# First gate unit taken into the last recurrence head, and early splitting of the merged tiles

## The chip, the cores and the metric

One core of one Trainium2 chip runs the whole program. The metric is device time in microseconds (us) of one execution. The kernel drives its five engines by hand: TensorE (PE in the rows, its weight loads PEld), VectorE (DVE), ScalarE (ACT), GpSimd (POOL) and SyncE (SP, which only starts transfers). Each engine has its own instruction stream; the streams meet through semaphores. Matmul results go to PSUM, of which there are 8 banks of 512 fp32 columns on 128 partitions.

## The reference

One layer of a decoder trunk over 1088 tokens (T: a prompt of L = 1024, and 8 samples of 8) with model width 1024 (KD = 8 tiles of 128 channels). What matters here is the part between the recurrence and the output projection:

```python
# token_mixer, cut
hq, hf, hi, hg, fq, fk, fv, ff, mg = jnp.split(h @ lw['w_in'], SPLIT_IDX, axis=-1)
o_h, s_new = hgrn_chunked(...)                      # 4 heads, state 128x128
o_h = rmsnorm(o_h, lw['hg_onorm']) * jax.nn.silu(hg)
br_h = o_h.reshape(B, L, HG_WIDTH) @ lw['w_br_h']   # 512 -> 1024
...
br_f = o_f.reshape(B, L, FOX_WIDTH) @ lw['w_br_f']  # 512 -> 1024
g_h, g_f = jnp.split(jax.nn.sigmoid(mg), N_BRANCH, axis=-1)
y = (g_h * br_h + g_f * br_f) @ lw['w_out']
```

Around it, `layer` computes the modulation `mod = silu(c) @ ada_w + ada_b` for 9 conditions, two norms, and a squared-ReLU MLP. Everything is fp32.

## The kernel before, in words

Activations lie channel-major: a tile is 128 channels by 1088 tokens. An fp32 product is made from three products of split operands, high x high, low x high and high x low. ScalarE makes a high part by a copy to fp32r (`split_hi`, L255), VectorE a low part by a subtraction (`split_lo`, L261). The projection from `w_in` is cut into **units** of 128 output channels: 8 k-tiles, each of 9 matmuls (3 products in 3 column pieces), 72 matmuls at L273 in `channel_tile`. Weights of a unit are loaded by SP into `w_raw` (two slots, L449), split into `w_hi` and `w_lo` (two slots), and the result stands in one of two accumulators: `acc(0)` lies in PSUM banks 0 to 2, `acc(1)` in banks 3 to 5. Semaphores count units: `w_hi_ready`, `w_lo_ready`, `unit_done` (PE), `acc_read` (the accumulator was read).

The program has phases with a barrier between them (`phase_end`: the engine drains, raises its count, and, unless `wait=False`, waits for the other three).

**Phase 4, the recurrence**: 4 heads (`head`). In a head, PE projects units 1 to 3 of the head, transposes, runs the chunked recurrence (L1933 to L1966), then, in the heads 0 to 2, projects the first unit of the next head, while ACT sums the squares of the last token block, DVE (L1462), POOL (L730, the power -0.5) and DVE again (L1464, L1466) make the norm and raise `hn_ready`. Then PE transposes the normed tokens into bank 2 and banks 6 and 7 (L1975, L1977), and DVE multiplies them with the output gate into `mix` (L1473, 64 and 1024 columns). The last head (`last_one=True`) has no next unit and projects nothing there. POOL stores the states by DMA and waits for that before it ends its phase.

**Phase 5, the merge** (`merge_pair` on PE, ACT and DVE): 8 steps `d`, one for each channel tile, in pairs `it` with `dd` 0 and 1; three pairs in a loop (`Fori`), the last one written out. A step on PE is: gate unit 0 (for `g_h`) into `acc(0)`, branch product 0 (`br_h`, L2026) into `acc(1)`, gate unit 1 (`g_f`) into `acc(0)`, branch product 1 into `acc(1)`, and a small transpose (L2043). After each half of a gate unit comes a `mod_pair` (L2001), small matmuls for the modulation, whose weights POOL loads in 512 KB pieces into two buffers (L758); piece i is loaded when piece i-2 was used. `gate` begins with

```python
pe.wait_ge(w_lo_ready, n + 1)
pe.wait_ge(w_hi_ready, n + 1)
pe.wait_ge(acc_read, n)        # every accumulator before this one was read
```

ACT applies the sigmoid (L1034), DVE multiplies the branch product with it (L1501) and adds the two (L1503) into `merged[:, d]`. Before the first step PE waits for all engines' phase 4 and for `c_spread`, which POOL raises after it has started four branch-weight transfers (L746, L747) and spread the conditions (L753).

**End of phase 5**: after the last step ACT copies the eight merged tiles to `h_hi` (L1051), DVE subtracts for `h_lo` (L1516, `merged_split`). `h_hi` and `h_lo` hold the input of the gate units until then. PE starts phase 6 without a barrier: the output projection (L2057, `out_step`) takes k-tile by k-tile for the first four token tiles (s = 0 to 3: 6 matmuls of 512 columns each; y of tile s stands in banks 2s and 2s+1), and for each k waits for `merged_split` and the split weights. The weights of k = 0 and 1 are split ahead; those of k = 2 to 7 are split by ACT and DVE in phase 6, after the barrier, and k = 4 to 7 are loaded by SP after it, between the loads of x and of the norm rows (L507 to L513).

**Lines that the prediction's steps touch**: `merge_pair` of ACT, DVE and PE, `head` of DVE and PE, `gate`, `branch`, the loop over k of the output projection.

Of the kernel before, what the change touches and what calls it, by code (L numbers as in the profile page):

```python
# [15 lines left out]
F32 = mybir.dt.float32  # L16
# [4 lines left out]
ACT = mybir.ActivationFunctionType  # L21
# [8 lines left out]
def build_layer(nc, x_prompt, x_sample, c_prompt, c_sample, cache_k, cache_v, cache_logf, state_hgrn, page_table,  # L30
# [8 lines left out]
    KD = D // P  # L39
# [53 lines left out]
    with ExitStack() as ctx:  # L93
# [739 lines left out]
        def _(act):  # L833
# [159 lines left out]
            with act.Fori(0, HH) as h:  # L993
                hi(U_HG, 4, h, 1)
                act.wait_ge(unit_done, 4 * h + (U_HG + 1))
                a0 = acc(U_HG % 2)
                ACTIVATE(hK, a0, ACT.Sigmoid, scale=-1.0)
                ACTIVATE(hF, a0, ACT.Sigmoid)
                act.drain().then_inc(acc_read, 1)
                hi(U_HG, 4, h, 2)  # L1000
                act.wait_ge(unit_done, 4 * h + (U_HG + 2))
                ACTIVATE(hQ, acc((U_HG + 1) % 2), ACT.Copy, scale=float(DK) ** -0.5).then_inc(acc_read, 1)
                act.wait_ge(f_ready, h + 1)
                ACTIVATE(hF, hF, ACT.Ln).then_inc(g_ready, 1)
                hi(U_HG, 4, h, 3)
                act.wait_ge(unit_done, 4 * h + (U_HG + 3))
                ACTIVATE(hV, acc(U_HG % 2), ACT.Copy).then_inc(acc_read, 1)
                act.wait_ge(b_ready, h + 1)
                ACTIVATE(hE, hB, ACT.Exp)
                ACTIVATE(hN, hB, ACT.Exp, scale=-1.0)  # L1010
                act.drain().then_inc(eb_ready, 1)
                hi(U_HG, 4, h, 4)
                act.wait_ge(unit_done, 4 * h + (U_HG + 4))
                ACTIVATE(hS, acc((U_HG + 1) % 2), ACT.Silu).then_inc(acc_read, 1)
                for t in range(NT + 1):
                    r = P if t < NT else TS
                    act.wait_ge(ho_ready, (NT + 1) * h + t + 1)
                    ACTIVATE(h_otok[0:r, t, :], bank(4 + t % 2 if t < NT else 6, 0, P, rows=r), ACT.Copy).then_inc(ho_copied, 1)
                    act.drain()
                    ACTIVATE(hF[0:r, P * (t % 2):P * (t % 2) + P], h_otok[0:r, t, :],  # L1020
                             ACT.Square, accum_out=h_ms[0:r, t:t + 1])
                act.drain().then_inc(hss_ready, 1)
            phase_end(act, "act", 4)


            act.sem_inc(mod_copied, 1)

            def merge_pair(it, last=False):
                for dd in range(2):
                    for j, dst in enumerate((gate_h, gate_f)):  # L1030
                        hi(U_MG, 4, it, 2 * dd + j + 1)
                        n, slot, _ = number(U_MG, 4, it, 2 * dd + j)
                        act.wait_ge(unit_done, n + 1)
                        ACTIVATE(dst, acc(0), ACT.Sigmoid).then_inc(acc_read, 1)  # L1034
                    if last and dd:
                        hi(U_OUT, 0, 0, 1)
                        act.wait_ge(rows_tr, 1)
                        ACTIVATE(rows_T, bank(7, P, 4 * P, rows=KD * NC), ACT.Copy)
                        act.drain()
                        act.dma_start(rows_dram[:, 0:3, :], rows_T.rearrange("p (v x) -> p v x", x=P))\  # L1040
                            .then_inc(rows_stored, 16)
                    act.wait_ge(ada_used, 8 * it + (KD + 4 * dd + 4))
                    act.wait_ge(mod_tr, 2 * it + dd + 1)
                    ACTIVATE(mod_cols, bank(6, 0, P), ACT.Copy).then_inc(mod_copied, 1)
                    act.wait_ge(br_added, 2 * it + dd + 1)

            with act.Fori(0, KD // 2 - 1) as it:
                merge_pair(it)
            merge_pair(KD // 2 - 1, last=True)
            for d in range(KD):  # L1050
                ACTIVATE(h_hi[:, d, :], merged[:, d, :], ACT.Copy).then_inc(h_raw, 1)  # L1051
            phase_end(act, "act", 5)


# [96 lines left out]
        def _(dve):  # L1151
# [246 lines left out]
            def head(h, last=False):  # L1398
# [66 lines left out]
                                h_ms[:, 0:NT].unsqueeze(2).broadcast_to([P, NT, DV]), ALU.mult)  # L1465
                v.tensor_scalar(h_otok[0:TS, NT, :], h_otok[0:TS, NT, :], h_ms[0:TS, NT:NT + 1], None, ALU.mult)  # L1466
                dve.drain().then_inc(hn_ready, 1)
                if not last:
                    lo(U_HG, 4, h, 5)
                mixed_head = mix[:, bass.ds(h + G, 1), :].rearrange("p a b -> p (a b)")  # L1470
                for i, (a, b, src) in enumerate(((L, T, bank(2, 0, TS)), (0, L, psum[:, 3072:3072 + L]))):
                    dve.wait_ge(ho_tr, 2 * h + i + 1)
# [10 lines left out]
            dve.sem_inc(mod_added, 1)  # L1483
            dve.sem_inc(br_read, 1)

            def merge_pair(it, last=False):
                for dd in range(2):
                    d = 2 * it + dd
                    lo(U_MG, 4, it, 2 * dd + 1)
                    lo(U_MG, 4, it, 2 * dd + 2)  # L1490
                    dst = merged[:, bass.ds(d, 1), :].rearrange("p a b -> p (a b)")
                    if last and dd:
                        times_norm(post1, 2, V_P1, False)
                        times_norm(pre2, 4, V_N2, True)
                        dve.drain().then_inc(rows_calc, 1)
                    for j, (out, gate) in enumerate(((dst, gate_h), (gate_f, gate_f))):
                        if last and dd and j:
                            lo(U_OUT, 0, 0, 1)
                        dve.wait_ge(acc_read, 4 * it + (U_MG + 2 * dd + j + 1))
                        dve.wait_ge(br_ready, 4 * it + (2 * dd + j + 1))  # L1500
                        v.tensor_mul(out, acc(1), gate).then_inc(br_read, 1)  # L1501
# [9 lines left out]
            with dve.Fori(0, KD // 2 - 1) as it:  # L1511
                merge_pair(it)
            merge_pair(KD // 2 - 1, last=True)
            for d in range(KD):
                dve.wait_ge(h_raw, KD + d + 1)
                v.tensor_sub(h_lo[:, d, :], merged[:, d, :], h_hi[:, d, :].bitcast(F32)).then_inc(merged_split, 1)  # L1516
            phase_end(dve, "dve", 5)


# [140 lines left out]
        def _(pe):  # L1660
# [249 lines left out]


            pe.wait_ge(hg_zeroed, 1)
            def head(h, last_one=False):
                for j in range(1, 4):
                    n, slot, _ = number(U_HG, 4, h, j)
                    project(pe, n, slot)
# [49 lines left out]
                    last = mm(bank(6, 0, P, rows=TS), q_by_b[:, b, :], s_states[:, b, :], start=False,  # L1966
                              stop=(b == NB - 1))
                last.then_inc(ho_ready, 1)
                if not last_one:
                    pe.wait_ge(ho_copied, (NT + 1) * h + NT)  # L1970
                    n, slot, _ = number(U_HG, 4, h, 4)
                    project(pe, n, slot)
                pe.wait_ge(hn_ready, h + 1)
                past_waits(pe, "pe")
                tr(bank(2, 0, TS), h_otok[0:TS, NT, :], ident[0:TS, 0:TS]).then_inc(ho_tr, 1)  # L1975
# [5 lines left out]
            project(pe, U_HG, U_HG % 2)  # L1981
            with pe.Fori(0, HH - 1) as h:
                head(h)
            head(HH - 1, last_one=True)
            phase_end(pe, "pe", 4)


            pe.wait_ge(c_spread, 1)
            pe.sem_inc(mod_tr, 1)

            def merge_pair(it, last_pair=False):
                for dd in range(2):
                    d = 2 * it + dd
                    def mod_pair(i):
# [10 lines left out]
                    def gate(j):  # L2005
# [5 lines left out]
                        for k in range(KD):  # L2011
                            last = channel_tile(slot, 0, k)
                            if k == KD - 1:
                                last.then_inc(unit_done, 1)
                            if k % 4 == 3:
                                mod_pair(2 * j + k // 4)

                    def branch(j):

                        w_br = br_raw[dd].rearrange("p (k n) -> p k n", n=P)  # L2020
                        if j == 0:
                            pe.wait_ge(br_landed[dd], 32 * it + 32)
                        pe.wait_ge(br_read, 4 * it + (2 * dd + j + 1))
                        for k in range(4):
                            for a, b in PIECES:
                                last = mm(acc(1)[:, a:b], w_br[:, 4 * j + k, :], mix[:, (G, 0)[j] + k, a:b],  # L2026
                                          start=(k == 0), stop=(k == 3))
                        last.then_inc(br_ready, 1)

                    gate(0)  # L2030
                    branch(0)
                    gate(1)
                    if last_pair and dd:
                        pe.wait_ge(mod_added, d + 1)
                        pe.wait_ge(rows_calc, 1)
# [6 lines left out]
                    pe.wait_ge(mod_added, d + 1)  # L2042
                    tr(bank(7, 0, P), mod_cols, ident[:, :]).then_inc(mod_tr, 1)  # L2043

            with pe.Fori(0, KD // 2 - 1) as it:
                merge_pair(it)
            merge_pair(KD // 2 - 1, last_pair=True)
            phase_end(pe, "pe", 5, wait=False)
# [25 lines left out]
            for k in range(KD):  # L2074
                pe.wait_ge(merged_split, k + 1)
                pe.wait_ge(w_lo_ready, U_OUT + k + 1)
                pe.wait_ge(w_hi_ready, U_OUT + k + 1)
                for s in range(4):
                    last = out_step(s, k)
                    if k == KD - 1:  # L2080
                        last.then_inc(y_ready, 1)
# [158 lines left out]
```

## Time and profile before

| | us |
|---|---|
| median of 3 runs | 2102.8 (2092.35 to 2103.53) |
| the profiled execution, timed | 2101.83 |
| its span in the trace | 2100.3 |
| PE busy in the span | 1940.7 (92%) |
| recurrence and merge (phases 4 and 5) | about 519 to 1186 |
| output projection and second norm (phase 6) | about 1191 to 1330 |
| MLP and finish | about 1330 to 2100 |

The profiled execution was timed 1.5 us above its own span and 1.0 us below the median. All times in the rows are counted from the span's start. A row of the timeline has: start, duration, engine, line, operation, output<-input, and in brackets how long the engine had been idle and what ended that. PEclk is the clock that TensorE was granted, in parts of its full 2.4 GHz; 0.50 is 1.2 GHz.

### The profile page before, as it was taken

The page shows a single profiled execution, that of the slowest core. Times are in us where ns is not written, and L with a number is a line of the kernel's source. Part 1 is how long each engine was busy: PE and PEld are TensorE (multiplying, and loading weights), DVE is VectorE, ACT ScalarE, POOL GpSimd, SP SyncE. Part 2 cuts the span into 40 slices and gives each one's busy share as a digit, 9 for nine tenths or more (in the row PEclk, how much of TensorE's full clock was granted, in tenths as well). Part 3 has the DMA queues.
Part 4 walks back from the last instruction along what each step waited for, and adds up shares of the span by engine and source line. Part 5 has one row for each costly group of instructions (what it writes and reads, how often), then busy time and mean ns, then how long its engine had stood idle before and what let it go on. Part 6 is the DMA issues. An engine that isn't in the chain of part 4 may idle for free.

```text
span 2100.3 us, 32236 instructions
## 1 busy us (share of the span) xinstructions
PE 1940.7 (92%) x12640; PEld 1623.1 (77%) x12640; DVE 715.9 (34%) x975; ACT 612.6 (29%) x878; POOL 406.7 (19%) x442
## 2 busy tenths in 40 slices
PE   4988988687999997899999999999999999999996
PEld 2777867455877875677777678899999999999976
DVE  3634244453345455021111346323132222313235
ACT  5545345232233332111111233222222322223221
POOL 2212021233011012110010033230211213030203
PEclk9999999898999999899999999999999999999998
DMA  7101011396110211333223243111111111111132
GB/s 277 40 24 42 21 42 32 128 312 234 34 42 20 61 42 32 100 92 99 80 80 91 79 141 107 49 50 43 48 40 50 40 49 41 40 50 40 50 115 86
DMA packets 136556, 159.80 MB, mean 76 GB/s; under 512 B 9625, under 2 KB 110282, under 8 KB 135322
## 3 DMA queue, kind: packets, MB, share of 16 engines
q1 hardware_dynamic: 118288, 104.65, 16.1%
q0 software_dynamic: 15936, 46.97, 7.4%
q10 hardware_dynamic: 2250, 7.04, 1.0%
q8 instruction: 57, 0.93, 0.2%
q14 instruction: 25, 0.20, 0.0%
HBM read 142.72 MB, written 15.91 MB: 76 GB/s over the span
## 4 chain that ended last, share of the span: by engine, by line
PE 80%; DVE 6%; issue 5%; ACT 3%; DMA 2%; POOLq 1%; POOL 1%; DVEq 1%; PEld 1%; ACTq 0%; SPq 0%; PEldq 0%
PE psum L273 41%; PE psum L2159 16%; PE psum L2026 6%; PE psum L2057 4%; PE psum L1771 2%; DVE work L1446 2%; PE psum L1784 1%; DVE nmax L1288 1%; ACT work L945 1%; PE psum L2108 1%; PE psum L1852 1%; PE psum L1846 1%; PE psum L2001 1%; DMA work<-in_cache_k 1%; DMA work<-in_cache_v 1%
## 5 line engine op out<-in xcount | busy, mean ns | idle before, releaser
L273 PE MATMUL psum<-h_hi,w_hi 128*128 128x288 f32 (+1 forms) x1776 | 400.1, 334 | 16.1 <-POOL work L753 10.1
L273 PE MATMUL psum<-h_hi,w_lo 128*128 128x288 f32 (+1 forms) x1776 | 392.8, 330 | 0.0
L273 PE MATMUL psum<-h_lo,w_hi 128*128 128x288 f32 (+1 forms) x1776 | 392.8, 330 | 0.0
L273 PEld LDWEIGHTS psum<-h_hi,w_hi 128*128 128x128 f32 x1776 | 270.0, 190 | 51.9 <-issue 24.0
L261 DVE TENSOR_TENSOR w_lo<-w_raw,w_hi 128x1024 fp32r<-128x1024 f32 x108 | 164.9, 1526 | 402.5 <-ACT w_hi L255 395.4
L273 PEld LDWEIGHTS psum<-h_lo,w_hi 128*128 128x128 f32 x1776 | 270.3, 189 | 26.3
L273 PEld LDWEIGHTS psum<-h_hi,w_lo 128*128 128x128 f32 x1776 | 270.1, 189 | 26.3
L812 POOL TENSOR_TENSOR work<-work 128x1088 f32<-128x1088 f32 x56 | 142.2, 2540 | 505.8 <-ACTq L1128 505.8
L2159 PE MATMUL psum<-u_hi,w_hi 128*128 128x288 f32 (+1 forms) x672 | 148.7, 329 | 0.0
L2159 PE MATMUL psum<-u_lo,w_hi 128*128 128x288 f32 (+1 forms) x672 | 147.8, 328 | 0.0
L2159 PE MATMUL psum<-u_hi,w_lo 128*128 128x288 f32 (+1 forms) x672 | 147.2, 327 | 0.0
L255 ACT ACTIVATE w_hi<-w_raw 128x1024 fp32r<-128x1024 f32 x108 | 113.8, 1053 | 60.3 <-DVEq L1504 48.7
L1127 ACT ACTIVATE work<-psum 128x1088 f32<-128x1088 f32 x56 | 60.4, 1079 | 232.5 <-PE psum L2159 232.5
L1606 DVE TENSOR_TENSOR work<-work 128x1088 f32<-128x1088 f32 x32 | 41.4, 1293 | 247.1 <-ACTq L1112 247.1
L2026 PE MATMUL psum<-mix,work 128*128 128x288 f32 (+1 forms) x384 | 121.2, 472 | 0.0
L1111 ACT ACTIVATE work<-psum 128x1088 f32<-128x1088 f32 x32 | 34.6, 1081 | 273.1 <-PE psum L273 264.9
L2159 PEld LDWEIGHTS psum<-u_hi,w_hi 128*128 128x128 f32 x672 | 102.2, 188 | 9.4
L2159 PEld LDWEIGHTS psum<-u_lo,w_hi 128*128 128x128 f32 x672 | 101.3, 188 | 10.3
L2159 PEld LDWEIGHTS psum<-u_hi,w_lo 128*128 128x128 f32 x672 | 101.1, 188 | 10.2
L2026 PEld LDWEIGHTS psum<-mix,work 128*128 128x128 f32 x384 | 71.6, 190 | 45.3 <-issue 33.6
L1034 ACT ACTIVATE work<-psum 128x1088 f32<-128x1088 f32 x16 | 17.2, 1077 | 226.1 <-PE psum L273 226.1
L1501 DVE TENSOR_TENSOR work<-psum,work 128x1088 f32<-128x1088 f32 (+1 forms) x16 | 20.7, 1292 | 180.8 <-PE psum L2026 180.8
(361 smaller groups left out, 2403.2 us busy)
## 6 DMA issues: line engine op xcount, KB each, us to landing
w_raw<-in_w_in SPq DMA_DIRECT2D x44, 512.0 KB, 3.9
work<-in_cache_k SPq DMA_DIRECT2D x64, 256.0 KB, 6.4
work<-in_cache_v POOLq DMA_DIRECT2D x64, 256.0 KB, 5.1
work<-in_ada_w POOLq DMA_DIRECT2D x32, 512.0 KB, 4.0
w_raw<-in_w_mlp_up SPq DMA_DIRECT2D x32, 512.0 KB, 4.0
w_raw<-in_w_mlp_down SPq DMA_DIRECT2D x32, 512.0 KB, 3.5
work<-in_ada_w SPq DMA_DIRECT2D x8, 1024.0 KB, 16.2
out<-work POOLq DMA_DIRECT2D x12, 512.0 KB, 4.0
```

Of the source, the lines that this page charges most:

```text
L255: nc.scalar.activation(w_hi[:, slot, :] if home is None else home, w_raw[:, slot, :], ACT.Copy)\
L261: nc.vector.tensor_sub(low, w_raw[:, slot, :], high.bitcast(F32)).then_inc(w_lo_ready, 1)
L273: last = nc.tensor.matmul(out[:, a:b], w, m[:, k, a:b], start=(k == 0 and w is wh and m is h_hi), stop=(k == KD - 1 and w is wl))
L812: nc.gpsimd.tensor_add(yT[:, j, :], yT[:, j, :], down[j % 2]).then_inc(down_free, 1)
L1111: ACTIVATE(relu[j % 2], acc((U_MLP + j) % 2), ACT.Relu).then_inc(acc_read, 1)
L1127: ACTIVATE(down[i], acc((U_MLP + i) % 2), ACT.Copy).then_inc(acc_read, 1)
L1446: v.scalar_tensor_tensor(states[(c + 1) % 8], states[c % 8], hE[:, end:end + 1], bank(t % 2, P * i, P * i + P), ALU.mult, ALU.add)\
L1606: v.tensor_mul(usq, relu[j % 2], relu[j % 2])
L1771: last = mm(bank(6, 0, P)[rows, :], f_vtok[:, kb, rows], probsT[j][:, kb, :], start=(kb == 0), stop=(kb == i))
L2026: last = mm(acc(1)[:, a:b], w_br[:, 4 * j + k, :], mix[:, (G, 0)[j] + k, a:b], start=(k == 0), stop=(k == 3))
L2057: last = mm(psum[0:token_rows(s), y_out(s) + a:y_out(s) + a + 512], m[:, k, tok], w[:, a:a + 512], start=(k == 0 and m is h_hi and w is ou ...
L2159: product = mm(out[:, a:b], w, m[:, k, a:b], start=(k == 0 and w is wh and m is u_hi), stop=(k == UT - 1 and w is wl))
```

## The change

Two things. First, PE's last head projects the first gate unit (unit U_MG, into `acc(1)`) where the other heads project their next unit; the high part of unit U_MG+1 is made by ACT at its end of phase 4, the low part by DVE inside the last head. PE no longer waits for the barrier after phase 4: it goes on to `gate(1)` of the first step without the modulation pairs, and only then waits for `c_spread` and the other engines' phase 4, runs modulation pairs 0 and 1, branch 0 (into `acc(0)`), pairs 2 and 3, branch 1. The first pair is written out for this, and the loop runs over two pairs. Second, in the last step ACT copies seven of the eight tiles to `h_hi` after its modulation copy and before it waits for the last addition, DVE subtracts the first three of them before its last branch multiplication, and PE waits for that multiplication and for the last modulation sum only when it comes to token tiles 1 and 3 of k = 0.

```diff
 ACT
                 act.drain().then_inc(hss_ready, 1)
+            hi(U_MG, 0, 0, 1)
             phase_end(act, "act", 4)
...
-                        hi(U_MG, 4, it, 2 * dd + j + 1)
+                        if not (first and dd == 0 and j == 0):
+                            hi(U_MG, 4, it, 2 * dd + j + 1)
                         n, slot, _ = number(U_MG, 4, it, 2 * dd + j)
                         act.wait_ge(unit_done, n + 1)
-                        ACTIVATE(dst, acc(0), ACT.Sigmoid).then_inc(acc_read, 1)
+                        ACTIVATE(dst, acc(1 if first and dd == 0 and j == 0 else 0), ACT.Sigmoid).then_inc(acc_read, 1)
...
                     ACTIVATE(mod_cols, bank(6, 0, P), ACT.Copy).then_inc(mod_copied, 1)
+                    if last and dd:
+                        for d in range(KD - 1):
+                            ACTIVATE(h_hi[:, d, :], merged[:, d, :], ACT.Copy).then_inc(h_raw, 1)
                     act.wait_ge(br_added, 2 * it + dd + 1)
...
-            for d in range(KD):
-                ACTIVATE(h_hi[:, d, :], merged[:, d, :], ACT.Copy).then_inc(h_raw, 1)
+            ACTIVATE(h_hi[:, KD - 1, :], merged[:, KD - 1, :], ACT.Copy).then_inc(h_raw, 1)
 DVE
-                if not last:
-                    lo(U_HG, 4, h, 5)
+                lo(U_HG, 4, h, 5)
...
+            def merged_low(d):
+                dve.wait_ge(h_raw, KD + d + 1)
+                v.tensor_sub(h_lo[:, d, :], merged[:, d, :], h_hi[:, d, :].bitcast(F32)).then_inc(merged_split, 1)
...
                         if last and dd and j:
                             lo(U_OUT, 0, 0, 1)
+                            for e in range(3):
+                                merged_low(e)
                         dve.wait_ge(acc_read, 4 * it + (U_MG + 2 * dd + j + 1))
                         dve.wait_ge(br_ready, 4 * it + (2 * dd + j + 1))
-                        v.tensor_mul(out, acc(1), gate).then_inc(br_read, 1)
+                        v.tensor_mul(out, acc(j if first and dd == 0 else 1), gate).then_inc(br_read, 1)
...
-            for d in range(KD):
-                ...
+            for d in range(3, KD):
+                merged_low(d)
 PE
-                if not last_one:
-                    pe.wait_ge(ho_copied, (NT + 1) * h + NT)
-                    n, slot, _ = number(U_HG, 4, h, 4)
-                    project(pe, n, slot)
+                pe.wait_ge(ho_copied, (NT + 1) * h + NT)
+                n, slot, _ = number(U_HG, 4, h, 4)
+                project(pe, n, slot)
...
-            phase_end(pe, "pe", 4)
-            pe.wait_ge(c_spread, 1)
-            pe.sem_inc(mod_tr, 1)
+            phase_end(pe, "pe", 4, wait=False)
...
-                    gate(0)
-                    branch(0)
-                    gate(1)
+                    if first_pair and dd == 0:
+                        gate(1, pairs=False)
+                        pe.wait_ge(c_spread, 1)
+                        pe.sem_inc(mod_tr, 1)
+                        for e in ("act", "dve", "pool"):
+                            pe.wait_ge(done_of[e], 4)
+                        mod_pair(0)
+                        mod_pair(1)
+                        pe.wait_ge(acc_read, U_MG + 2)
+                        branch(0)
+                        mod_pair(2)
+                        mod_pair(3)
+                    else:
+                        if first_pair:
+                            pe.wait_ge(br_read, 2)
+                        gate(0)
+                        branch(0)
+                        gate(1)
...
-            with pe.Fori(0, KD // 2 - 1) as it:
+            merge_pair(0, first_pair=True)
+            with pe.Fori(1, KD // 2 - 1) as it:
                 merge_pair(it)
...
                 for s in range(4):
+                    if k == 0 and s == 1:
+                        pe.wait_ge(br_read, 1 + 2 * KD)
+                    if k == 0 and s == 3:
+                        pe.wait_ge(mod_added, 1 + KD)
                     last = out_step(s, k)
```

## Rows read from the trace of the kernel before

**Rows 1.** What PE waited for, 760 to 900 us: total, times, longest.

```profile
PE psum L273 <- POOL work L753: 10.1, 1, 10.1
PE psum L1975 <- DVEq L1467: 6.2, 1, 6.2
```

**Rows 2.** Timeline, end of the last head and start of the merge.

```profile
828.75 1.96 PE L1966 MATMUL psum<-work 128*64 128x128 f32 x16
...
836.90 0.34 PE L1975 MATMUL psum<-ident,work 64*128 64x64 f32 x1 [6.18 <-DVEq L1467]
...
837.16 1.97 PE L1977 MATMUL psum<-ident,work 128*128 128x128 f32 x8
...
839.17 1.28 DVE L1473 SCALAR_TENSOR_TENSOR mix<-psum,vec,work 128x1024 f32<-128x1024 f32 x1 [1.62 <-PE psum L1977]
841.32 1.28 ACT L255 ACT_TABLE_LOAD   x1 [9.82 <-POOLq L243]
...
848.66 1.43 POOL L758 DMA_DIRECT2D work<-in_ada_w  x2 [0.17 <-issue]
...
849.20 1.27 PE L273 MATMUL psum<-h_hi,w_hi 128*128 128x288 f32 x3 [10.07 <-POOL work L753]
```

**Rows 3.** Timeline of ACT: the first sigmoid of the merge.

```profile
863.67 1.08 ACT L1034 ACTIVATE work<-psum 128x1088 f32<-128x1088 f32 x1 [18.70 <-PE psum L273]
```

**Rows 4.** Chain that ended last (start, us, what): head 2, merge step 0, output projection.

```profile
755.86 12.35 PE psum L273 x72
769.43 35.58 PE psum L273 x216
...
849.20 7.67 PE psum L273 x36
857.44 6.19 PE psum L273 x36
864.21 7.51 PE psum L2026 x24
...
892.74 6.00 PE psum L273 x36
...
1191.34 43.35 PE psum L2057 x174
```

**Rows 5.** Timeline, end of the merge and start of the output projection.

```profile
1180.60 0.28 ACT L1044 ACTIVATE work<-psum 128x128 f32<-128x128 f32 x1 [0.50 <-issue]
...
1186.11 1.29 DVE L1501 TENSOR_TENSOR work<-psum,work 128x1088 f32<-128x1088 f32 x1 [5.13 <-PE psum L2026]
...
1188.85 8.11 ACT L1051 ACTIVATE h_hi<-work 128x1088 fp32r<-128x1088 f32 x8 [7.98 <-DVEq L1504]
1188.91 0.20 DVE L1507 TENSOR_TENSOR mod<-psum,vec 128x36 f32<-128x36 f32 x1
1189.99 9.71 DVE L1516 TENSOR_TENSOR h_lo<-work,h_hi 128x1088 fp32r<-128x1088 f32 x8 [0.89 <-ACT h_hi L1051]
...
1191.34 1.22 PE L2057 MATMUL psum<-w_hi,h_hi 128*128 128x512 f32 x2 [5.23 <-DVE h_lo L1516]
```

**Rows 6.** Stretches: length, PE PEld DVE ACT POOL busy (count), PEclk, DMA share, GB/s.

```profile
516.20:519.30 3.10, 0.00 (x0) 0.00 (x0) 0.37 (x2) 2.36 (x3) 2.10 (x8) 0.79 0.00 0
519.40:524.40 5.00, 5.00 (x17) 4.51 (x18) 1.22 (x1) 1.16 (x1) 0.90 (x1) 0.50 0.50 132
...
849.20:852.40 3.20, 3.20 (x11) 2.91 (x12) 0.00 (x0) 0.00 (x0) 0.89 (x2) 0.50 0.75 214
...
1191.30:1197.10 5.80, 5.76 (x14) 4.50 (x15) 5.80 (x5) 5.67 (x6) 0.00 (x0) 0.50 0.00 0
```

**Rows 7.** Timeline of DVE: low parts of w_out for k = 2 and k = 7.

```profile
1201.03 1.23 DVE L261 TENSOR_TENSOR u_hi<-w_raw,u_hi 128x1024 fp32r<-128x1024 f32 x1 [1.32 <-ACT u_hi L255]
...
1226.67 1.22 DVE L261 TENSOR_TENSOR work_r<-w_raw,work_r 128x1024 fp32r<-128x1024 f32 x1 [4.50 <-ACT work_r L255]
```

**Rows 8.** The page, part 3, instruction transfers: packets, MB, share of 16 engines.

```profile
q8 instruction: 57, 0.93, 0.2%
```

More of the change, by code:

```diff
@@ L1022, in _, with merge_pair @@
                 act.drain().then_inc(hss_ready, 1)
+            hi(U_MG, 0, 0, 1)
             phase_end(act, "act", 4)
             act.sem_inc(mod_copied, 1)
-            def merge_pair(it, last=False):
+            def merge_pair(it, first=False, last=False):
                 for dd in range(2):
                     for j, dst in enumerate((gate_h, gate_f)):
-                        hi(U_MG, 4, it, 2 * dd + j + 1)
+                        if not (first and dd == 0 and j == 0):
+                            hi(U_MG, 4, it, 2 * dd + j + 1)
                         n, slot, _ = number(U_MG, 4, it, 2 * dd + j)
                         act.wait_ge(unit_done, n + 1)
-                        ACTIVATE(dst, acc(0), ACT.Sigmoid).then_inc(acc_read, 1)
+                        ACTIVATE(dst, acc(1 if first and dd == 0 and j == 0 else 0), ACT.Sigmoid).then_inc(acc_read, 1)
                     if last and dd:
@@ L1044, in merge_pair @@
                     ACTIVATE(mod_cols, bank(6, 0, P), ACT.Copy).then_inc(mod_copied, 1)
+                    if last and dd:
+                        for d in range(KD - 1):
+                            ACTIVATE(h_hi[:, d, :], merged[:, d, :], ACT.Copy).then_inc(h_raw, 1)
                     act.wait_ge(br_added, 2 * it + dd + 1)
-            with act.Fori(0, KD // 2 - 1) as it:
+            merge_pair(0, first=True)
+            with act.Fori(1, KD // 2 - 1) as it:
                 merge_pair(it)
             merge_pair(KD // 2 - 1, last=True)
-            for d in range(KD):
-                ACTIVATE(h_hi[:, d, :], merged[:, d, :], ACT.Copy).then_inc(h_raw, 1)
+            ACTIVATE(h_hi[:, KD - 1, :], merged[:, KD - 1, :], ACT.Copy).then_inc(h_raw, 1)
             phase_end(act, "act", 5)
@@ L1484, in _, with merge_pair @@
             dve.sem_inc(br_read, 1)
-            def merge_pair(it, last=False):
+            def merged_low(d):
+                dve.wait_ge(h_raw, KD + d + 1)
+                v.tensor_sub(h_lo[:, d, :], merged[:, d, :], h_hi[:, d, :].bitcast(F32)).then_inc(merged_split, 1)
+            def merge_pair(it, first=False, last=False):
                 for dd in range(2):
                     d = 2 * it + dd
-                    lo(U_MG, 4, it, 2 * dd + 1)
+                    if not (first and dd == 0):
+                        lo(U_MG, 4, it, 2 * dd + 1)
                     lo(U_MG, 4, it, 2 * dd + 2)
@@ L1509, in merge_pair @@
                         .then_inc(mod_added, 1)
-            with dve.Fori(0, KD // 2 - 1) as it:
+            merge_pair(0, first=True)
+            with dve.Fori(1, KD // 2 - 1) as it:
                 merge_pair(it)
             merge_pair(KD // 2 - 1, last=True)
-            for d in range(KD):
-                dve.wait_ge(h_raw, KD + d + 1)
-                v.tensor_sub(h_lo[:, d, :], merged[:, d, :], h_hi[:, d, :].bitcast(F32)).then_inc(merged_split, 1)
+            for d in range(3, KD):
+                merged_low(d)
             phase_end(dve, "dve", 5)
@@ L1912, in _, with head @@
             pe.wait_ge(hg_zeroed, 1)
-            def head(h, last_one=False):
+            def head(h):
                 for j in range(1, 4):
@@ L1983, in _, with merge_pair @@
                 head(h)
-            head(HH - 1, last_one=True)
-            phase_end(pe, "pe", 4)
-            pe.wait_ge(c_spread, 1)
-            pe.sem_inc(mod_tr, 1)
-            def merge_pair(it, last_pair=False):
+            head(HH - 1)
+            phase_end(pe, "pe", 4, wait=False)
+            def merge_pair(it, first_pair=False, last_pair=False):
                 for dd in range(2):
@@ L2003, in mod_pair, with gate @@
                         last.then_inc(ada_used, 1)
-                    def gate(j):
+                    def gate(j, pairs=True):
                         n, slot, _ = number(U_MG, 4, it, 2 * dd + j)
@@ L2014, in gate @@
                                 last.then_inc(unit_done, 1)
-                            if k % 4 == 3:
+                            if pairs and k % 4 == 3:
                                 mod_pair(2 * j + k // 4)
@@ L2022, in branch @@
                             pe.wait_ge(br_landed[dd], 32 * it + 32)
-                        pe.wait_ge(br_read, 4 * it + (2 * dd + j + 1))
+                        if not (first_pair and dd == 0):
+                            pe.wait_ge(br_read, 4 * it + (2 * dd + j + 1))
                         for k in range(4):
                             for a, b in PIECES:
-                                last = mm(acc(1)[:, a:b], w_br[:, 4 * j + k, :], mix[:, (G, 0)[j] + k, a:b],
+                                last = mm(acc(j if first_pair and dd == 0 else 1)[:, a:b], w_br[:, 4 * j + k, :], mix[:, (G, 0)[j] + k, a:b],
                                           start=(k == 0), stop=(k == 3))
                         last.then_inc(br_ready, 1)
-                    gate(0)
-                    branch(0)
-                    gate(1)
+                    if first_pair and dd == 0:
[16 more added lines that the diff above has]
+                        gate(1)
                     if last_pair and dd:
```

## The prediction

> **What bounds the kernel now.** The page comes first: PE is busy for 92% of the span, and from about 1330 us on it runs the MLP without gaps. A change to another engine pays only where PE stands still, so the second view is the list of what PE waited for. From 760 to 900 us it has two long entries [rows 1]: 6.2 us for the end of the norm in the last head, and 10.1 us for POOL's spreading of the conditions, after the barrier. The timeline shows what fills them [rows 2]. PE finishes the recurrence at 830.71 (828.75 + 1.96), stands until 836.90, runs the transposes until 839.13, and stands until 849.20. The reader is to see that no engine works throughout these gaps; they are chains of short steps and waits. The third place is the end of the merge [rows 5]: PE starts the output projection at 1191.34, 5.23 us after its last transpose (1186.11), after a multiplication, an addition, ACT's first copy and DVE's first subtraction, one behind the other.
>
> The idle time has a second price. After the gaps, rows of stretches give PE a granted clock of 0.50, the 1.2 GHz level [rows 6]: 3.2 us from 849.2, 5.8 us from 1191.3, and 5.0 us from 519.4 after an idle stretch of 3.1 us. Work done there would have taken half as long at the full level, so these cost 1.6, 2.9 and 2.5 us.
>
> **Part 1, the gate unit in the last head.** Total PE work stays; what is gained is idle time. Before, from the end of the recurrence (830.71) to the first matmul of step 1 (892.74) it takes 62.0 us [rows 2, 4]. After, by steps:
>
> - The unit in the gap: head 2 does just this in 12.35 us, from 755.86, and its transposes take 1.22 us more, to 769.43 [rows 4]. In the last head they took 2.2 us, at half clock [rows 2]. Here: 830.71 + 12.35 + 1.22 = 844.3. The norm chain (hn_ready at 836.9) lies under the unit, and so does DVE's extra low part, 1.23 us as in rows 7, and ACT's extra high part, which follows its squares at about 832. SP's loads need only splits that are ready earlier.
> - The new wait. PE skips the barrier, but the following gate unit still waits until every earlier accumulator is read, so for the sigmoid of the unit just made, and ACT reaches that only behind its own barrier. The barrier ends with DVE's large product, 1.28 us after the transposes [rows 2], at 845.65 with its drain; POOL's state transfers were done by 841.3, when ACT passed the barrier [rows 2]. Behind it I put a table load of 1.28 us, as ACT had one right after this barrier in rows 2 (from below: none), and the sigmoid of 1.08 us [rows 3]; with some 0.2 us of semaphores PE starts at 848.25. That is 3.95 us of idle time.
> - Gate unit 1: 6.00 + 6.19 = 12.2 us (a first half at full clock, the row at 892.74, and a second half, the row at 857.44, in [rows 4]). After 3.95 us of idle time I take half clock, which rows 6 show behind idle stretches of 3.1, 5.2 and 10.1 us, at the mean of the three prices, 2.3 us. The ends are 0 (full clock kept) and 2.9. It ends at 862.8.
> - Four modulation pairs at 0.57 us (849.20 + 7.67 to 857.44 in rows 4), 2.3 us; two branch products of 7.51 us [rows 4], 15.0; the small transpose 0.1. Branch 0 needs the second sigmoid, 1.08 us: it lies under pairs 0 and 1.
>
> Sum: 848.25 + 12.2 + 2.3 + 2.3 + 15.0 + 0.1 = 880.2, so 12.5 us gained.
>
> What lies behind the covers: POOL now passes the barrier at 845.8 instead of 841.3, and starts the first modulation transfers 848.66 - 841.3 = 7.4 us later, at 853.2. How long they take is bounded by 8.1 us, the time from 848.66 to their use behind 856.87 [rows 2, 4], and from below by 0; by the upper end they are there at 861.3, 1.5 us early. Pair 2 is loaded once pair 0 is done, at 863.4, and used at 871.5: by the same 8.1 us just in time. So 0, with this as the thinnest cover. Branch 0 goes into the other accumulator; DVE reads it while PE runs pairs 2, 3 and branch 1, so the new wait ahead of step 1 is over in time: 0.
>
> For the table load, the row shows 1.28 us. The Trainium skill's page "ScalarE: Activation LUTs", section "Table sets: the hidden batching unit", counts about 2.7 us for one; by that the sum would be 1.4 us smaller. The row decides.
>
> **Part 2, the merged tiles.** ACT's modulation copy ends at 1180.88 [rows 5]; the seven copies follow at 8.11/8 = 1.01 us each, the first three ready by 1184.0. DVE's three subtractions (9.71/8 = 1.21 us) are then done at 1185.3 to 1185.7. The multiplication they stand in front of is released at 1186.11 [rows 5]: a cover of 0.4 us or more; were it gone, PE would wait at token tile 1 by as much. PE begins k = 0 at 1186.15. Its first token tile takes a quarter of 5.6 us, 1.4 us, to 1187.55; the multiplication ends at 1187.40, so tile 1 finds it done. Tile 3 begins at 1190.3, the modulation sum ends at 1189.11 [rows 5]. The gap of 5.23 us and the 2.9 us of half clock go: 8.1 us.
>
> What is late next: DVE's other five subtractions run from 1189.1 to 1195.2, and with them the barrier comes 4.5 us earlier than 1199.70 (1189.99 + 9.71). The split of w_out for k = 2 was done 2.56 us behind it (1202.26, [rows 7]), now at 1197.8; PE wants it after two k-tiles of 5.6 us, at 1197.35. That costs 0.5 us. For k = 7 the split is done at 1227.89 [rows 7]; PE needs it 1.4 us before 1234.69 (1191.34 + 43.35, [rows 4]), at 1233.3. The cover of 5.4 us shrinks to about 2.2, since the weights come 4.4 us earlier and PE 7.6. So part 2 brings 7.6 us. Its lower end is 5.4, if those loads come no earlier at all; its upper end 8.1.
>
> **The sum**: 12.5 + 7.6 = 20.1 us. As a check, gaps and half clock that go: 6.2 + 10.1 + 5.2 + 1.6 + 1.0 + 2.9 = 27.0; those that come: 3.95 + 2.3 + 0.5 = 6.8; the difference is 20.2. The rest of the kernel moves as one piece, as it is bound by PE or starts from PE's results. The profiled execution took 2101.8, which makes 2081.7; the median shown is 1.0 above that execution. I predict **2082 us**. The unknown costs carry the gain from 17.3 (half clock 2.9, part 2 at 5.4) to 23.7 (full clock kept, no table load, 8.1), that is 2078 to 2085.
>
> **Rivals.**
>
> *PE waits as long as before.* The change says PE goes on past the barrier, but the accumulator wait holds it. If ACT's barrier came as late behind the transposes as POOL's chain did, 10.07 us instead of 3.95, or the modulation transfers missed their cover by as much, part 1 would bring 6.4 us and the whole 14: 2088. For it speaks that the wait is there and that the pairs stand close together; against, that DVE's 1.28 us is the only work left before the barrier. Chance 0.14.
>
> *Little of it arrives.* If also the output projection's weights became the bound and the three subtractions held up the multiplication, both parts would lose their covers: 6.4 + 4 at most, about 2092 or above, no change that can be told. A measurement of this kernel can tell about 0.5%, 10.5 us, from no change. Chance 0.10, the spread of the runs (one of three lay 10.4 us below the median) counted in.
>
> *Slower: code that comes late.* The first pair is now written out beside the loop, in three engines' streams. If new code had to be waited for, its place would be PE's stream from 844 to 930 us. The price: 57 packets of instructions took 0.2% of 16 engines' span, about 1.2 us each [rows 8]. To end slower by 0.5% some 30 us must be lost, 25 packets in series, nearly half of all those of the program. Against it: the last head, written out too, ran its recurrence to 830.71, 61.3 us after its first unit [rows 2, 4], without such a gap. The Trainium skill's page "Runtime: NRT & Kernel Launch", section "Instruction fetch mechanics", says that crossing a block of code is mostly hidden; the trace agrees. Chance 0.04.
>
> **How the numbers follow.** The forecast has 0.72. The range reaches to the first rival and a little beyond, 2091, where about 0.15 is left out; downward to 2072, for the 23.7 us and part of the spread of the runs. Faster by over 0.5%: 0.72 + 0.14 = 0.86; within: 0.10; slower: 0.04.
>
> **What would show it.** In the profile of the changed kernel: 72 matmuls of L273's form between the recurrence and the transposes of the last head; one PE gap of about 4 us, released by ACT's sigmoid, with a table load in front of it; half clock behind that gap, and none at the output projection, which follows the last transpose at once and stops for half a microsecond at k = 2. A PE gap in front of modulation pair 0 or 2, released by a transfer, or one at token tile 1, would say that a cover was thinner than read. The prediction is wrong if the new gap is near 10 us, or if the output projection's gain is lost again before the MLP.

## The result and the profile after

The changed kernel takes 2083.06 us (median of 8 runs, 2074.46 to 2091.28), the kernel before 2100.67 us (8 runs, 2092.35 to 2110.74). The ratio is 0.9922, its 95% interval 0.9894 to 0.9949: faster by 0.8%, between 0.5% and 1.1%. The forecast was 2082 us.

The profiled execution of the changed kernel is the slowest of its eight: 2091.28 us, span 2089.8 us. Its span is only 10.5 us shorter than that of before, although its stages show twice as much, so it is read stage by stage. **Stage A** runs from the end of the last recurrence to the first gate matmul of merge step 1, **stage B** from the end of PE's last transpose of the merge to the first MLP unit after the output projection. Both are counted by the rows of the chain; the MLP runs from the start of its first up matmul to the start of its last.

| | before | after | change |
|---|---|---|---|
| stage A | 62.0 | 49.1 | -12.9 |
| merge steps 1 to 7 | 293.4 | 293.4 | 0 |
| stage B | 143.95 | 136.6 | -7.35 |
| MLP, first to last up matmul | 691.5 | 700.8 | +9.3 |
| tail | 78.7 | 81.7 | +2.9 |
| everything ahead of stage A | 830.7 | 828.2 | -2.5 |

The last three rows scatter from execution to execution. The change leaves the code ahead of stage A as it was, and in the twelve profiles of this document that stretch takes 825.2 to 834.4 us; the tail takes 78.2 to 82.3 us, and the MLP is taken up behind the experiments.

First, what PE waited for from 760 to 900 us in the changed kernel (total, times, longest):

```profile
PE psum L273 <- ACT work L1036: 4.0, 1, 4.0
...
PE psum L2034 <- ACT work L1036: 0.2, 1, 0.2
```

The two entries of [rows 1] are gone. One of 4.0 us is new, released by the sigmoid. The timeline, from the end of the recurrence, shows how it comes about:

```profile
826.28 1.96 PE L1977 MATMUL psum<-work 128*64 128x128 f32 x16
...
840.36 0.27 PE L1985 MATMUL psum<-ident,work 64*128 64x64 f32 x1
...
840.57 1.09 PE L1987 MATMUL psum<-ident,work 128*128 128x128 f32 x8
...
841.70 1.28 DVE L1477 SCALAR_TENSOR_TENSOR mix<-psum,vec,work 128x1024 f32<-128x1024 f32 x1 [0.74 <-PE psum L1987]
...
843.12 1.28 ACT L1036 ACT_TABLE_LOAD   x1 [12.74 <-DVEq L243]
...
844.42 1.08 ACT L1036 ACTIVATE work<-psum 128x1088 f32<-128x1088 f32 x1
...
850.72 1.43 POOL L758 DMA_DIRECT2D work<-in_ada_w  x2 [0.16 <-issue]
859.92 1.08 PE L2008 MATMUL psum<-work 128*32 128x128 f32 x32
...
861.16 7.58 PE L2034 MATMUL psum<-mix,work 128*128 128x288 f32 x24 [0.16 <-ACT work L1036]
```

PE now works where [rows 2] had the first gap, then DVE's product, ACT's table load and the sigmoid follow one another. The chain of waits gives the lengths, to be held against [rows 4]:

```profile
828.24 12.19 PE psum L273 x72
841.70 1.28 DVE mix L1477
843.21 1.21 issue
845.64 14.37 PE psum L273 x72
861.16 7.58 PE psum L2034 x24
869.75 7.51 PE psum L2034 x24
877.37 5.99 PE psum L273 x36
```

The unit behind the gap takes 14.37 us, the one before it 12.19. The stretches (columns as in [rows 6]) say why: the clock is at 0.50 for 4.6 us, at 1.00 after that, and it is at 1.00 at the start of the output projection too, where [rows 6] had 0.50.

```profile
841.80:845.50 3.70, 0.00 (x0) 0.00 (x0) 1.18 (x1) 2.36 (x3) 1.81 (x3) 0.73 0.08 18
845.70:850.30 4.60, 4.60 (x15) 4.12 (x16) 1.23 (x1) 0.74 (x1) 1.34 (x4) 0.50 0.89 253
850.40:857.00 6.60, 6.60 (x42) 6.01 (x42) 0.00 (x0) 0.00 (x0) 1.58 (x3) 1.00 0.63 200
1171.00:1177.00 6.00, 6.00 (x27) 4.96 (x28) 5.78 (x6) 2.60 (x3) 0.00 (x0) 1.00 0.01 3
```

The end of the merge, to be held against [rows 5], in the timeline:

```profile
1165.38 7.10 ACT L1049 ACTIVATE h_hi<-work 128x1088 fp32r<-128x1088 f32 x7
...
1166.52 3.69 DVE L1492 TENSOR_TENSOR h_lo<-work,h_hi 128x1088 fp32r<-128x1088 f32 x3 [0.93 <-ACT h_hi L1049]
1170.46 0.27 PE L2066 MATMUL psum<-ident,work 128*128 128x128 f32 x1
1170.73 1.29 DVE L1512 TENSOR_TENSOR work<-psum,work 128x1088 f32<-128x1088 f32 x1 [0.51 <-PE psum L2034]
1170.99 0.70 PE L2081 MATMUL psum<-w_hi,h_hi 128*128 128x512 f32 x2 [0.27 <-issue]
...
1182.38 1.17 PE L2081 MATMUL psum<-u_hi,h_hi 128*128 128x512 f32 x4 [0.25 <-issue]
```

The three subtractions end at 1170.2, half a microsecond before the multiplication is released; the output projection follows the transpose after 0.27 us, and stops once more for 0.25 us at k = 2. Stage B ends with the first MLP unit, which the chains have at these times, before and after:

```profile
1330.06 25.79 PE psum L273 x144
```

```profile
1307.33 26.05 PE psum L273 x144
```

### The profile page after: what moved, and what is told of

The parts are those of the page before. It is cut to its first block, busy times and chain, and to the rows that moved or that the text cites. A ratio compares the mean times of both kernels' runs of the same rounds, so it can differ in the third digit from the quotient of the medians.

```text
span 2089.8 us, 32193 instructions
## 1 busy us (share of the span) xinstructions
PE 1945.3 (93%) x12640; PEld 1623.5 (78%) x12640; DVE 716.3 (34%) x975; ACT 606.2 (29%) x873; POOL 405.8 (19%) x442
## 4 chain that ended last, share of the span: by engine, by line
PE 82%; DVE 6%; issue 4%; ACT 3%; DMA 1%; POOLq 1%; POOL 1%; DVEq 1%; PEld 1%; ACTq 0%; PEldq 0%; SPq 0%
PE psum L273 42%; PE psum L2187 16%; PE psum L2034 6%; PE psum L2081 4%; PE psum L1782 2%; DVE work L1451 2%; PE psum L1863 1%; PE psum L1795 1%; PE psum L1857 1%; DVE nmax L1293 1%; ACT work L945 1%; PE psum L2136 1%; PE psum L2008 1%; DVE work L1349 1%; PE psum L2208 1%
## 5 line engine op out<-in xcount | busy, mean ns | idle before, releaser
L273 PEld LDWEIGHTS psum<-h_hi,w_hi 128*128 128x128 f32 x1776 | 270.7, 190 | 47.3 <-issue 17.6
```

Of the source, the lines that this page charges most:

```text
L273: last = nc.tensor.matmul(out[:, a:b], w, m[:, k, a:b], start=(k == 0 and w is wh and m is h_hi), stop=(k == KD - 1 and w is wl))
```

## The experiments

Theory: the change is worth the idle time of PE that it takes away, stage by stage, with the half clock behind it. Each experiment says which stage must move. Six of the ten runs below are single executions; the eight of the changed kernel lie 16.8 us apart, so the single ones are read by their stages alone, and a ratio is given where there were several.

**Part 1 alone.** The changed kernel with the splitting put back behind the last addition.

```diff
-                    if last and dd:
-                        for d in range(KD - 1):
-                            ACTIVATE(h_hi[:, d, :], merged[:, d, :], ACT.Copy).then_inc(h_raw, 1)
...
-            ACTIVATE(h_hi[:, KD - 1, :], merged[:, KD - 1, :], ACT.Copy).then_inc(h_raw, 1)
+            for d in range(KD):
+                ACTIVATE(h_hi[:, d, :], merged[:, d, :], ACT.Copy).then_inc(h_raw, 1)
...
-                            for e in range(3):
-                                merged_low(e)
...
-                    if k == 0 and s == 1:
-                        pe.wait_ge(br_read, 1 + 2 * KD)
-                    if k == 0 and s == 3:
-                        pe.wait_ge(mod_added, 1 + KD)
```

> Stage A is counted from the end of the last head's recurrence to the first gate matmul of merge step 1 (62.0 us before, 49.1 after); stage B from PE's last transpose of the merge to the first MLP unit after the output projection (143.95 us before, 136.6 after). Theory (two independent gains, each the PE idle time of its own stage): stage A 49.1 within 1 us, stage B back at 144 within 1 us with a PE gap of 5.2 us and half clock behind it; the whole about 12.9 us below the kernel before. Rival (the earlier start of the merge is given back behind it, so that both parts are needed together): stage A 49, but the merge body longer than 293.4 us or the whole under 6 us faster.

Stage A 48.5, stage B 143.7, ratio to the kernel before 0.9951 (0.9929 to 0.9973), which is 10.3 us, between 5.7 and 14.9. In what PE waited for, the gap of [rows 5] is back:

```profile
PE psum L273 <- ACT work L1036: 4.0, 1, 4.0
...
PE psum L2077 <- DVE h_lo L1490: 5.2, 1, 5.2
```

**Part 2 alone.** The kernel before with the early copies, the three early subtractions and PE's two waits.

```diff
+                        for d in range(KD - 1):
+                            ACTIVATE(h_hi[:, d, :], merged[:, d, :], ACT.Copy).then_inc(h_raw, 1)
...
+                            for e in range(3):
+                                merged_low(e)
...
+                    if k == 0 and s == 1:
+                        pe.wait_ge(br_read, 1 + 2 * KD)
+                    if k == 0 and s == 3:
+                        pe.wait_ge(mod_added, 1 + KD)
```

> Theory: stage A as before (62.0, half clock of the gate unit's start may move it by 1 us), stage B 136.6 within 1 us; the whole about 7.4 us faster, no more than the scatter of single runs. Rival (the output projection's gain comes from the shifted weight loads of the merge, not from the early split): stage B stays near 144.

Stage A 62.3, stage B 136.65, ratio 0.9978 (0.9954 to 1.0003), which is 4.6 us. So the parts are independent: each moves its own stage alone by what it moves it with the other, within 0.6 us, and the merge steps between take 293.6 to 293.7 us in all twelve profiles, counted from the first matmul of step 1 to the end of the last transpose. The timed ratio of part 2 alone takes in 1; its 7.3 us are shown by the stage, not by the timed runs.

**The unit moved, the barrier kept.**

```diff
-                        gate(1, pairs=False)
                         pe.wait_ge(c_spread, 1)
                         pe.sem_inc(mod_tr, 1)
                         for e in ("act", "dve", "pool"):
                             pe.wait_ge(done_of[e], 4)
+                        gate(1, pairs=False)
                         mod_pair(0)
```

> The gate unit moved into the last head, but PE waits for the barrier and for c_spread in front of gate unit 1. Theory: only the first gap of before (6.2 us) is filled; a gap of 8.5 to 10 us released by POOL stands behind the transposes, stage A 55 to 56 us, 6 us more than with the wait skipped. Rival (the accumulator wait holds PE as long as the barrier did): stage A 49 to 50 us.

Stage A 55.7, with one long wait, which is the second one of [rows 1] again:

```profile
PE psum L273 <- POOL work L753: 9.1, 1, 9.1
```

So of the 12.9 us about half is the unit in the first gap (6.3), the other half the barrier that PE skips (6.6). The split is not sharp. In this execution the granted clock was already low as the recurrence ended (0.69 on average from 826.0 to 833.7 us, 0.53 from there to 835.8), and the unit in the gap took longer than the 12.19 us of the changed kernel:

```profile
833.74 13.09 PE psum L273 x72
```

So some 0.9 us of the 6.6 are not the barrier's; the wait itself is 5.1 us longer with the barrier than without. The first rival of the prediction, that the accumulator wait holds PE as long as the barrier did, falls: it holds PE for 4.0 us, not 9.1.

**No subtraction, and seven, ahead of the multiplication.**

```diff
-                            for e in range(3):
-                                merged_low(e)
...
-            for d in range(3, KD):
+            for d in range(KD):
                 merged_low(d)
```

```diff
-                            for e in range(3):
+                            for e in range(7):
                                 merged_low(e)
...
-            for d in range(3, KD):
+            for d in range(7, KD):
                 merged_low(d)
```

> The early copies of ACT kept, but no subtraction ahead of DVE's last branch multiplication. Theory: PE waits for multiplication, addition, modulation sum and the first subtraction, 4.2 us behind the last transpose, and finds half clock behind that as before, 1.5 to 2.9 us: stage B 141 to 144 us. Rival (the early copies are the gain, the subtractions lie off PE's path): stage B 137 us.

> Seven subtractions ahead of DVE's last branch multiplication instead of three. Theory (the multiplication stands behind them, and PE waits for it in front of token tile 1): subtractions until about 19.9 us after ACT's modulation copy began... in numbers of the trace after: first at 1166.5, seven by 1.23 us to 1175.2, multiplication to 1176.5 instead of 1172.0; PE waits 4.1 us at token tile 1, perhaps with half clock behind: stage B 140.5 to 143 us. Rival (DVE is off PE's path there): 136.6.

Stage B 141.5 and 141.7 us. What PE waited for, without subtractions ahead, then with seven:

```profile
PE psum L2079 <- DVE h_lo L1492: 4.2, 1, 4.2
```

```profile
PE psum L2081 <- DVE work L1512: 3.7, 1, 3.7
```

With none, PE waits for the first subtraction, which stands behind the addition; with seven it waits at token tile 1 for the multiplication, which stands behind the subtractions. Either way stage B is 4.9 to 5.1 us longer than with three. So the subtraction and the multiplication both stand on PE's path, and three are enough for the first and few enough for the second; other numbers between none and seven were not run.

**The gap filled.** 16 matmuls whose result is thrown away.

```diff
+                        pe.wait_ge(w_hi_ready, U_MG + 2)
+                        for _ in range(16):
+                            mm(bank(0), w_hi[:, (U_MG + 1) % 2, 0:P], h_hi[:, 0, 0:512], start=True, stop=True)
                         gate(1, pairs=False)
```

> 16 matmuls whose result is thrown away (512 columns each, 0.22 us) put into PE's remaining gap in front of gate unit 1, in the accumulator which that unit starts anew. They compute nothing of the reference. Theory (the idle time itself costs the clock): the granted clock stays at 1.00, gate unit 1 takes 12.2 us instead of 14.4, and stage A 46.9 us. Rival (the clock falls there for another reason, or the fill delays the unit): 49 us or more.

Stage A 47.2, 1.9 us less than with the gap empty. The chain, and the stretch with the clock at 1.00:

```profile
838.90 3.92 PE psum L2041 x16
842.82 12.21 PE psum L273 x72
```

```profile
842.20:846.00 3.80, 3.80 (x23) 3.16 (x22) 1.23 (x1) 1.39 (x2) 1.94 (x4) 1.00 0.79 256
```

The idle time did cost the clock: with PE busy in its place it stayed at 1.00, and the next unit took 12.21 us instead of 14.37.

**The gap removed.** ACT waits for POOL alone in front of the first sigmoid, and a sigmoid of 128x1 numbers loads the table while ACT is idle.

```diff
             hi(U_MG, 0, 0, 1)
-            phase_end(act, "act", 4)
+            ACTIVATE(rinv[:, 0:1], ones[:, :], ACT.Sigmoid)
+            phase_end(act, "act", 4, wait=False)
+            act.wait_ge(done_of["pool"], 4)
...
+                        if first and dd == 0 and j == 0:
+                            act.wait_ge(done_of["pe"], 4)
+                            act.wait_ge(done_of["dve"], 4)
```

> ACT waits only for POOL's phase 4 in front of the first sigmoid, for PE's and DVE's behind it, and loads the sigmoid's table early, by a sigmoid of 128x1 numbers. Theory (the gap of 4 us is ACT's barrier, table load and sigmoid in a row, and half clock comes from it): the sigmoid ends as the transposes end, the gap is under 0.5 us, the clock stays full; gate unit 1 ends 6 us earlier, and now modulation pair 0 is late by 1 to 3 us, since POOL's transfers still start behind the barrier: stage A 44 to 46 us. Rival (something else holds gate unit 1, the weights or their splits): stage A 48 to 49 us.

A miss in the size: stage A 48.1 by the chain (47.9 where the next expectation counts to the first matmul itself), only 1.0 us less. The gap in front of the unit is gone, but another is there:

```profile
855.88 0.32 POOL L753 COPY work<-c_act 128x72 f32<-128x72 f32 x1 [5.23 <-issue]
856.35 1.43 POOL L758 DMA_DIRECT2D work<-in_ada_w  x2 [0.15 <-issue]
...
860.74 0.64 PE L2013 MATMUL psum<-work 128*32 128x128 f32 x16 [2.94 <-DMA work<-in_ada_w]
```

PE is now early and waits for a transfer, 2.9 us ahead of modulation pair 0 and 0.45 ahead of pair 1, and 3.4 us of half clock follow. Gate unit 1 did end 6.0 us earlier, counted from the recurrence (25.8 us against 31.8), and the late pair 0 was foreseen; left out was that its wait costs the clock again. So 5.0 of the 6.0 us went into the next wait and what follows it. POOL's step from the memset to the spreading, ahead of these transfers, took 5.2 us here (5.3 in the next kernel) against 3.3 in the changed kernel; why was not tried.

**The gap removed, and the work put in another order.** As in the last experiment, with branch 0 ahead of the modulation pairs, in the other accumulator.

```diff
-                        mod_pair(0)
-                        mod_pair(1)
-                        pe.wait_ge(acc_read, U_MG + 2)
                         branch(0)
+                        mod_pair(0)
+                        mod_pair(1)
+                        pe.wait_ge(acc_read, U_MG + 2)
+                        branch(1)
                         mod_pair(2)
                         mod_pair(3)
...
```

> As early_sigmoid (its stage A was 47.9 us: the gap in front of gate unit 1 had gone, but PE waited 2.9 us for the transfer of modulation pair 0 and ran 3.4 us at half clock behind that), with branch 0 put in front of modulation pairs 0 and 1 and into the accumulator of gate unit 0, branch 1 into the other, pairs 2 and 3 behind it. Theory (the transfers need only 3 us more cover, and the half clock comes from the wait): no PE gap over 0.7 us from the last head to step 1, clock 1.00 throughout, stage A 43.5 to 44.5 us, 4.5 to 5.4 us less than the changed kernel; whole 1.0 to 1.1 % below the kernel before. Rival (the wait moves to pairs 2 and 3 or to the small transpose): stage A 46 us or more.

Stage A 43.6, stage B 136.6; no PE gap over 0.4 us from the recurrence to step 1, and the clock, over the whole stretch:

```profile
834.00:877.00 43.00, 42.34 (x266) 33.23 (x265) 10.20 (x18) 6.45 (x9) 10.44 (x14) 1.00 0.37 112
```

Ratio to the kernel before 0.9888 (0.9849 to 0.9928). By its stages it is 5.5 us ahead of the changed kernel. Timed on the same chip the two were 2080.05 and 2082.94 us (medians of 6 runs); their intervals overlap, so the runs alone don't separate them.

**The changed kernel twice more**, unaltered, for its profile and for its time beside that.

> The changed kernel, unaltered, for one more profile. In its first profile every block of MLP up units took 48.64 us against 47.36 in the kernel before, though neither the code nor its inputs differ there; eight blocks make 10 us, the span less the stages A and B. Theory (the pace of the matmul stream is set anew in each execution, where PE last waited): blocks of 47.4, 48.0 or 48.6 us, with no tie to the kernel, and a span that follows it by 5 us a step. Rival (the written-out code has shifted the MLP's code, and made it slower): 48.64 again here and in every kernel with both parts.

> The changed kernel again, timed beside early_reordered on one chip. Theory: stage A 49, stage B 136.6, 0.8 % below the kernel before; its MLP blocks at 47.4 or at 48.6 us, whichever this execution draws. Rival (the gain of 0.8 % was the scatter of single executions): not below the kernel before by more than its interval.

Stages A and B as in the first profile (49.4 and 49.2; 136.6 both), ratio in the second case 0.99 (0.9861 to 0.9939), so the gain is more than the scatter. The chain of waits of the first has its MLP block of four up units at the length of before, that of the second at that of the first profile:

```profile
1764.41 47.36 PE psum L273 x288
```

```profile
1764.37 48.64 PE psum L273 x288
```

So the 9.3 us that the profiled execution lost in the MLP belong to the execution and not to the change. The rival, that shifted code made the MLP slower, falls. Of the theory not all came out: no MLP block took 48.0 us, the two lengths make a step of 9 to 11 us in the MLP and not of 5, and that PE's last wait sets the pace is not shown.

## Why the prediction was right, point by point

- *What bounds the kernel*: PE's idle time at three places. Right. The first place, filled alone, brought 6.3 us, the third, taken away alone, 7.3; the second was measured only as a difference (6.6 us, of which some 0.9 belong to one execution's clock). Filling the last gap with useless work gave back the clock.
- *The unit in the gap*, 12.35 + 1.22 us: 12.19 + 1.23.
- *The new wait*, 3.95 us, from DVE's product, a table load and the sigmoid: 3.98, in this order. The table load took 1.28 us. The Trainium skill's page "ScalarE: Activation LUTs", section "What ACT_TABLE_LOAD costs", puts a switch at about 2.66 us, 1.28 of them the load and the rest a drain. The load agrees; of a drain nothing shows here, since the load begins 0.14 us after DVE's product and the sigmoid 0.02 us after the load.
- *Half clock behind it*, 2.3 us in a range from 0 to 2.9: gate unit 1 took 14.37 us, 2.2 more than at full clock. In the six profiles that share this gap its price was 1.6 to 2.6 us (13.77 us in part 1 alone, 14.84 in the changed kernel's second profile).
- *Modulation pairs and branches*: the cover that was called the thinnest, pair 2, held; pair 0 too. Branch 0 waited 0.16 us for the second sigmoid, which had been put at 0. The prediction's worry about these transfers was well placed: once the 4 us gap was removed, PE waited 2.9 us for pair 0.
- *Sum of part 1*: 12.5 predicted, 12.9 measured.
- *The range*: the upper end of the gain adds up to 24.2 us, not 23.7 (12.5 + 2.3 + 1.28 + 8.1); the measured gain lies below both.
- *Part 2*: 7.6 predicted, 7.35 measured. PE's stops of 0.27 and 0.25 us stand where 0.04 and 0.5 were expected. The cover of the multiplication, 0.4 us or more, was 0.5.
- *"The rest of the kernel moves as one piece"*: this is the step that does not hold for a single execution. In the profiled pair the rest grew by 9.7 us (+9.3 + 2.9 - 2.5). Over the runs it is borne out within their scatter: the medians differ by 17.6 us, and the interval, 10.7 to 22.3 us, takes in the 20.3 us of the stages. That the forecast and the median lie 1 us apart is in part luck: the kernel before had a median of 2102.8 us in the three runs that the forecast started from and 2100.67 in eight, and the runs of the changed kernel lie 16.8 us apart. What bears the account out are the two stages.
- *The slower rival*, code that comes late: between 846 and 930 us, which takes in the written-out pair, PE has no gap but the 0.16 us ahead of branch 0. The row of [rows 8] went from 57 packets to 61.

## What to carry to other kernels

Where a matmul engine is the bound, count its idle time place by place, with the half clock that follows it, and put in the work that is ready; but look at once for the next wait in the engine's stream, since an accumulator that must first be read, or a transfer that starts behind the old barrier, keeps part of the old stop. A helper moved ahead of a critical instruction on its engine has a right number: too few leave the consumer waiting, too many hold up the critical one. Judge a change of one per cent by the stages in the trace, and by many runs; one execution against another says little.

## What the runs showed of the hardware

The same matmul stream ran at different paces in different executions. An MLP block of four up units (288 matmuls, rows of the chain of waits) took either 47.36 us, as in the kernel before, or 48.64 us, as in the changed kernel's first profile:

```profile
1784.24 47.36 PE psum L273 x288
```

```profile
1766.91 48.64 PE psum L273 x288
```

That is 164.4 against 168.9 ns for a matmul, at a granted clock of 1.00 in both. An execution keeps the pace from one block of up units to the next; the blocks of the down product between them take 47.79 us in all twelve profiles. The MLP as a whole took 690.0 to 691.5 us in seven of the twelve profiles and 700.8 us in five, and the three profiles of one and the same code (700.8, 691.5, 700.8) show both. This alone moves the time by 10 us, as much as the spread that the first runs show. The pace is not one of the whole execution, though. In the kernel before, three units of head 1 and the same three of head 2, one loop's code in one execution, took

```profile
613.33 35.80 PE psum L273 x216
692.28 36.73 PE psum L273 x216
```

which is 165.7 and 170.0 ns for a matmul, at a granted clock of 1.00 in both. Nor does the last head tell what the MLP will do: its three units took 36.51 us in the first two profiles of the changed kernel alike (from 765.47 and 768.19 us), and the MLP blocks behind them 48.64 and 47.36. What sets the pace stays open.
